# Three k pairs of each feed-forward down projection as seven block products

## What is computed

```python
def swiglu_ffn(h, w_in, w_out):
    g, u = jnp.split(h @ w_in, 2, axis=-1)
    return (jax.nn.silu(g) * u) @ w_out
...
    for l in range(DEPTH):
        x = x + 0.5 * swiglu_ffn(rmsnorm(x, norm_ffn1[l]), ffn1_w_in[l], ffn1_w_out[l])
        ...
        x = x + 0.5 * swiglu_ffn(rmsnorm(x, norm_ffn2[l]), ffn2_w_in[l], ffn2_w_out[l])
    return rmsnorm(x, norm_final)
```

## Time and profile before

| | us |
|---|---|
| median of three executions | 1100.32 (1100.07 to 1101.42) |
| the profiled execution, its own time | 1101.42 |
| its span, first to last instruction | 1099.6 |
| TensorE busy in the span | 1088.3 |
| VectorE busy | 727.4 |
| ScalarE busy | 547.6 |

### The profile page before, as it was taken

How to read it: one execution, slowest core, us unless ns; L and a number is a source line. 1 busy time by engine, 2 the same in 40 slices (tenths; PEclk the granted TensorE clock), 3 DMA queues, 4 the chain that set the end, 5 groups by cost and what they waited for, 6 DMA issues and landing times.

```text
span 1099.6 us, 14179 instructions
## 1 busy us (share of the span) xinstructions
PE 1088.3 (99%) x5350; PEld 919.9 (84%) x5350; DVE 727.4 (66%) x863; ACT 547.6 (50%) x616; POOL 394.8 (36%) x774
## 2 busy tenths in 40 slices
PE   8999999999999999999999999999999999999997
PEld 7878888889898888888888888888988988888886
DVE  6666556799776755655665665558997766666553
ACT  6453444854556545443454544357455645454432
POOL 0687632000000057673226858210000003686700
PEclk9999999999999999999999999999999999999999
DMA  8977566643553476765667776655455536766651
GB/s 277 290 226 230 181 205 210 213 170 134 210 192 114 142 224 216 219 213 204 210 205 218 217 222 201 203 198 196 149 178 184 175 121 193 216 216 221 204 192 66
DMA packets 183792, 215.92 MB, mean 196 GB/s; under 512 B 19088, under 2 KB 138540, under 8 KB 183724
## 3 DMA queue, kind: packets, MB, share of 16 engines
q1 hardware_dynamic: 158396, 200.55, 55.4%
q0 software_dynamic: 24064, 13.16, 4.4%
q10 hardware_dynamic: 1264, 1.32, 0.4%
HBM read 200.79 MB, written 1.05 MB: 184 GB/s over the span
## 4 chain that ended last, share of the span: by engine, by line
PE 93%; DMA 2%; DVE 2%; POOL 1%; ACT 1%; issue 1%; SPq 0%; ACTq 0%; DVEq 0%
PE acc L1497 26%; PE acc L1499 26%; PE acc L1498 26%; PE acc L1513 3%; PE acc L1514 3%; PE acc L1515 3%; PE turn L1374 2%; POOL kT L431 1%; DMA w_raw<-in_ffn_w_in 1%; DMA kT<-kT 1%; DVE w_lo L836 1%; ACT w_hi L470 1%; PE acc L1724 0%; PE acc L1723 0%; PE acc L1700 0%
## 5 line engine op out<-in xcount | busy, mean ns | idle before, releaser
L836 DVE TENSOR_TENSOR w_lo<-w_raw,w_hi 128x2048 fp32r<-128x2048 f32 (+1 forms) x190 | 426.0, 2246 | 194.9 <-ACT w_hi L470 194.8
L470 ACT CAST w_hi<-w_raw 128x2048 fp32r<-128x2048 f32 (+1 forms) x190 | 355.2, 1871 | 140.8 <-PE acc L1499 126.6
L431 POOL DMA_DIRECT2D kT<-kT x704 | 345.4, 499 | 161.6 <-DVE kT L968 120.8
L1497 PE MATMUL acc<-w_hi,xT 128*128 128x512 f32 x808 | 317.0, 392 | 0.7 <-DVE w_lo L836 0.6
L1499 PE MATMUL acc<-w_hi,xT 128*128 128x512 f32 x808 | 314.7, 390 | 0.0
L1498 PE MATMUL acc<-w_lo,xT 128*128 128x512 f32 x808 | 314.4, 389 | 0.0
L1497 PE MATMUL acc<-w_hi,hT 128*128 128x512 f32 x532 | 208.5, 392 | 0.0
L1499 PE MATMUL acc<-w_hi,hT 128*128 128x512 f32 x532 | 207.2, 390 | 0.0
L1498 PE MATMUL acc<-w_lo,hT 128*128 128x512 f32 x532 | 207.1, 389 | 0.0
L1497 PEld LDWEIGHTS acc<-w_hi,xT 128*128 128x128 f32 x808 | 151.7, 188 | 32.6 <-DVE w_lo L836 1.8
L1499 PEld LDWEIGHTS acc<-w_hi,xT 128*128 128x128 f32 x808 | 151.7, 188 | 31.8
(11 more groups left out here) (170 smaller groups left out, 951.9 us busy)
## 6 DMA issues: line engine op xcount, KB each, us to landing
w_raw<-in_ffn_w_in SPq DMA_DIRECT2D x172, 512.0 KB, 4.8
w_raw<-in_ffn_w_out SPq DMA_DIRECT2D x80, 512.0 KB, 4.4
w_raw<-in_mix_w_in SPq DMA_DIRECT2D x32, 512.0 KB, 4.5
w_raw<-in_xattn_wkv SPq DMA_DIRECT2D x32, 512.0 KB, 4.3
kT<-kT POOLq DMA_DIRECT2D x704, 16.0 KB, 3.3
w_raw<-in_mix_w_out SPq DMA_DIRECT2D x16, 512.0 KB, 4.4
w_raw<-in_xattn_wq SPq DMA_DIRECT2D x16, 512.0 KB, 4.6
w_raw<-in_xattn_wo SPq DMA_DIRECT2D x16, 512.0 KB, 4.5
```

Source lines behind the costliest of these rows:

```text
L431: pool.dma_start(hfeat[B * q:B * q + B, g % 2, a * RUN:(a + 1) * RUN], hblk[B * a:B * a + B, g % 2, q * RUN:(q + 1) * RUN]).then_inc(hfeat ...
L470: act.copy(w_hi[:, u % SLOTS, 0:n], w_raw[:, u % SLOTS, 0:n]).then_inc(w_split_hi, 1)
L836: dve.tensor_tensor(w_lo[:, u % SLOTS, 0:n], w_raw[:, u % SLOTS, 0:n], w_hi[:, u % SLOTS, 0:n].bitcast(F32), ALU.subtract).then_inc(w_spli ...
L1497: pe.matmul(o, hi, wh, start=(first and i == 0), stop=False)
```

## The change

For three pairs of k tiles (k 0 to 5) the two token tiles, the two k tiles and the two column halves make a 2 by 2 by 2 block product. Instead of eight block products (each three matmuls) seven are made, by Strassen's scheme in the form that shares sums. The list `DOWN` gives the new order of 15 units, here called D0 to D14 after their place in it: "singles" units hold two full weight rows of a pair (the four weight blocks, of which three are used directly, 9 matmuls), "sums" units hold four sums of blocks that VectorE makes out of the singles unit before (12 matmuls, no transfer), "rows" units are as before, with 4 or 2 k tiles. D1, D4 and D7 are singles, D2, D5 and D8 sums. All of n=0 ends with D9; n=1 is D10 to D14, with the two units of 2 k tiles as D11 and D12 and a unit of 4 k tiles last.

Sums over the tokens are made by VectorE in the first chunks (`token_sums`) and split by `sum_hi` and `sum_lo` into space of `xT` that is free after the in projection. The products that belong to several outputs are gathered by `shared_half`, `shares` and `last_shares`. The weight sums of the first pair stand in chunk 9, ahead of `hidden_lo`; in chunk 10 the block transpose now stands ahead of `split_lo` and `extra`.

```diff
+    SEVEN = 3
+    DOWN = [("rows", 0, 6, 4), ("singles", 0), ("sums", 0), ("rows", 0, 10, 4), ("singles", 1), ("sums", 1), ("rows", 0, 14, 4),
+            ("singles", 2), ("sums", 2), ("rows", 0, 18, 4), ("rows", 1, 6, 4), ("rows", 1, 18, 2), ("rows", 1, 20, 2),
+            ("rows", 1, 10, 4), ("rows", 1, 14, 4)]
+    U_MI = U_F1O + len(DOWN)
...
+            def square_parts(u, src, l, a):
+
+                return [(w_raw[:, u % SLOTS, i * 2 * GN:(i + 1) * 2 * GN], src[l, :, a + i, :]) for i in range(2)]
...
-                for n in range(2):
-                    for j in range(NGO):
-                        u = base + 2 * FC + n * NGO + j
-                        unit(u, at, wide_parts(u, src_out, l, GK * j, unit_kt(u), n * GN))
+                for i, e in enumerate(DOWN):
+                    u = base + 2 * FC + i
+                    if e[0] == "rows":
+                        unit(u, at, wide_parts(u, src_out, l, e[2], e[3], e[1] * GN))
+                    elif e[0] == "singles":
+                        unit(u, at, square_parts(u, src_out, l, 2 * e[1]))
+                    else:
+                        sp.wait_ge(w_split, at.at(UNITS, u + 1))
+                        sp.sem_inc(w_landed[u % SLOTS], 32)
...
+                f, e = down(u)
+                if e and e[0] == "sums":
+                    act.wait_ge(t_ready, at.at(2 * SEVEN, SEVEN * f + e[1] + 1))
+                else:
+                    act.wait_ge(w_landed[u % SLOTS], at.at(32 * (UNITS // SLOTS), 32 * (u // SLOTS + 1)))
                 act.wait_ge(unit_done, at.at(2 * UNITS, 2 * u + 2))
-                act.copy(w_hi[:, u % SLOTS, 0:n], w_raw[:, u % SLOTS, 0:n]).then_inc(w_split_hi, 1)
+                if e and e[0] == "singles":
+                    act.copy(w_hi[:, u % SLOTS, 0:GN], w_raw[:, u % SLOTS, 0:GN])
+                    act.copy(w_hi[:, u % SLOTS, 2 * GN:n], w_raw[:, u % SLOTS, 2 * GN:n]).then_inc(w_split_hi, 1)
+                else:
+                    act.copy(w_hi[:, u % SLOTS, 0:n], w_raw[:, u % SLOTS, 0:n]).then_inc(w_split_hi, 1)
...
+                    if c == FC - 1:
+                        sum_hi(0)
...
+                def sum_hi(p):
+                    at = Layer(l)
+                    act.wait_ge(s_sum_ready, at.at(2 * SEVEN, SEVEN * f + p + 1))
+                    act.wait_ge(unit_done, at.at(2 * UNITS, 2 * SLOTS + 2 * (base + 2 * FC - 1) + 2))
+                    act.copy(s_parts[p][:, :, 0, :], s_sum[p].rearrange("p (a s) -> p a s", a=2)).then_inc(s_hi_ready, 1)
+
                 for c in range(FC):
                     chunk(c, Layer(l))
-                split_hi(base + 2 * FC + 4, Layer(l))
+                state["next"] = base + 2 * FC + 4
+                for p in range(1, SEVEN):
+                    weights_to(base + 2 * FC + D_SUMS[p] - 1, Layer(l))
+                    sum_hi(p)
+                weights_to(base + 2 * FC + D_SUMS[-1], Layer(l))
...
+            def shared_half(f, at):
+
+                u = (U_F1O, U_F2O)[f] + D_SUMS[-1]
+                act.wait_ge(unit_done, at.at(2 * UNITS, 2 * SLOTS + 2 * u + 2))
+                act.wait_ge(s_ready, at.at(2 * SEVEN, SEVEN * f + SEVEN))
+                act.activation(shared, product_banks(f)[1][:, :], ACT.Copy, scale=0.5).then_inc(shared_ready, 1)
...
+                if e and e[0] == "singles" and e[1]:
+                    weight_sums(u, at)
...
+            def weight_sums(u, at):
+
+                w = w_raw[:, u % SLOTS, :].rearrange("p (i j n) -> p i j n", i=2, j=2)
+                s = w_raw[:, (u + 1) % SLOTS, :].rearrange("p (c n) -> p c n", c=4)
+                dve.wait_ge(w_landed[u % SLOTS], at.at(32 * (UNITS // SLOTS), 32 * (u // SLOTS + 1)))
+                dve.wait_ge(w_split, at.at(UNITS, SLOTS + u - 1))
+                steps.link(dve.tensor_tensor(s[:, 0:2, :], w[:, :, 1, :], w[:, 0, :, :], ALU.subtract))
+                steps.link(dve.tensor_tensor(s[:, 2, :], w[:, 1, 1, :], s[:, 0, :], ALU.subtract))
+                dve.tensor_tensor(s[:, 3, :], w[:, 1, 0, :], s[:, 2, :], ALU.subtract).then_inc(t_ready, 1)
...
-                    split_lo(base + 2 * c + 4, at)
-                    if (l, f) == (0, 0) and c in EXTRA:
-                        extra(EXTRA[c])
+                    def first_split():
+                        split_lo(base + 2 * c + 4, at)
+                        if (l, f) == (0, 0) and c in EXTRA:
+                            extra(EXTRA[c])
+
+                    if c < FC - 1:
+                        first_split()
...
+                    if c == FC - 2:
+                        weight_sums(base + 2 * FC + D_SUMS[0] - 1, at)
+                    if c == FC - 1:
+                        first_split()
+                        sum_lo(0)
...
+                    if c < SEVEN:
+                        token_sums(c, hfeat[:, g % 2, :].rearrange("p (a k t s) -> p k t a s", a=NBLK, k=2, t=T))
...
+                def token_sums(p, h):
+                    s = s_sum[p].rearrange("p (i a s) -> p i a s", i=4, a=NBLK)
+                    n = steps.mark(dve.tensor_tensor(s[:, 0, :, :], h[:, 0, 1, :, :], h[:, 1, 1, :, :], ALU.add))
+                    dve.tensor_tensor(s[:, 2, :, :], h[:, 0, 0, :, :], h[:, 0, 1, :, :], ALU.subtract)
+                    steps.wait(n)
+                    steps.link(dve.tensor_tensor(s[:, 1, :, :], s[:, 0, :, :], h[:, 0, 0, :, :], ALU.subtract))
+                    dve.tensor_tensor(s[:, 3, :, :], h[:, 1, 0, :, :], s[:, 1, :, :], ALU.subtract).then_inc(s_sum_ready, 1)
+
+                def sum_lo(p):
+                    dve.wait_ge(s_hi_ready, Layer(l).at(2 * SEVEN, SEVEN * f + p + 1))
+                    dve.tensor_tensor(s_parts[p][:, :, 1, :], s_sum[p].rearrange("p (a s) -> p a s", a=2),
+                                      s_parts[p][:, :, 0, :].bitcast(F32), ALU.subtract).then_inc(s_ready, 1)
+
                 for c in range(FC):
                     chunk(c, Layer(l))
-                split_lo(base + 2 * FC + 4, Layer(l))
+                state["next"] = base + 2 * FC + 4
+                for p in range(1, SEVEN):
+                    weights_to(base + 2 * FC + D_SUMS[p] - 1, Layer(l))
+                    sum_lo(p)
+                weights_to(base + 2 * FC + D_SUMS[-1], Layer(l))
                 hidden_lo(FC - 1)
-                state["next"] = base + 2 * FC + 5
...
+            def into_x(n, t, src, scalar):
+
+                o = xs[:, t, n * GN:(n + 1) * GN]
+                if scalar is None:
+                    return steps.mark(dve.tensor_tensor(o, src, o, ALU.add))
+                return steps.mark(dve.scalar_tensor_tensor(out=o, in0=src, scalar=scalar, in1=o, op0=ALU.mult, op1=ALU.add))
...
+            def shares(f, at):
+
+                u = (U_F1O, U_F2O)[f] + D_SUMS[-1]
+                m = product_banks(f)
+                dve.wait_ge(unit_done, at.at(2 * UNITS, 2 * SLOTS + 2 * u + 2))
+                dve.wait_ge(shared_ready, at.at(2, f + 1))
+                into_x(0, 0, shared, None)
+                steps.link(dve.scalar_tensor_tensor(out=shared_6, in0=m[6][:, :], scalar=0.5, in1=shared, op0=ALU.mult, op1=ALU.add))
+                steps.link(dve.scalar_tensor_tensor(out=shared, in0=m[7][:, :], scalar=0.5, in1=shared_6, op0=ALU.mult, op1=ALU.add))
+                steps.wait(into_x(0, 1, shared, None))
+
+            def last_shares(f):
+
+                m5 = product_banks(f)[5]
+                n = [into_x(1, 0, shared_6, None), into_x(1, 1, shared, None)]
+                for t in range(T):
+                    steps.wait(n[t])
+                    n[t] = into_x(1, t, m5[:, :], 0.5)
+                steps.wait(n[T - 1])
 
...
-                weights_to(U_F1O + 7, at)
-                update(0, 0, 0, U_F1O + 5, F1O_PAIR[0], 0.5, at)
-                update(0, 0, 1, U_F1O + 5, F1O_PAIR[0], 0.5, at)
+                weights_to(U_F1O + D_LAST[0] + 1, at)
+                shares(0, at)
+                weights_to(U_F1O + D_LAST[0] + 2, at)
+                update(0, 0, 0, U_F1O + D_LAST[0], F1O_PAIR[0], 0.5, at)
+                update(0, 0, 1, U_F1O + D_LAST[0], F1O_PAIR[0], 0.5, at)
                 for t in range(T):
                     x_blocks(2 * l, t)
-                weights_to(U_F1O + 11, at)
+                last_shares(0)
+                weights_to(U_MI, at)
                 gained_blocks(2 * l, G_MIX)
                 xT_lo_part(1, 0, 0, at)
                 xT_lo_part(1, 0, 1, at)
-                weights_to(U_MI, at)
-                update(0, 1, 0, U_F1O + 11, F1O_PAIR[1], 0.5, at)
+                update(0, 1, 0, U_F1O + D_LAST[1], F1O_PAIR[1], 0.5, at)
...
-                        ins = triple(acc[pair][t][:, :], u, j, t, 0, GN, False, t == 1 and j == GK - 1)
-                    ins.then_inc(unit_done, 1)
+                        ins = triple(acc[pair][t][:, :], u, j, t, 0, GN, False, False)
+                    if t == 0:
+                        ins.then_inc(unit_done, 1)
```

(67 more changed lines are left out.)

71 lines of the change are left out of this document (44 added, 27 removed).

## The result

The changed kernel takes 1103.6 us (median of 8, 1102.7 to 1105.7); the kernel before took 1100.9 us beside it on the same chip (8 runs, 1100.1 to 1101.4). The ratio is 1.0029, 95% interval 1.0020 to 1.0038. The forecast was 1095.9 us, with 1092.5 to 1099.8 as its range. The profiled execution took 1105.7 us, with a span of 1103.8 us against 1099.6. By the prediction's own sum the span should have shrunk by 4.4 us; it grew by 4.2, so 8.6 us have to be found.

A forecast was written before the change was run, and what follows sets the result against it. The prediction took TensorE's list of matmuls, busy 99% of the span, as the bound. Its terms, -8.2 + 2.6 + 1.8 + 0.1 - 0.7 = -4.4 us, gave 1095.9 us against the median of 1100.3, range 1092.5 to 1099.8.

The forecast's parts named there:

- No stall, but none to spare: At D3, D6 and D9, weight splits were to be ready in time, with margins of about 0.25 us.
- The landing that the prediction varied: Weight transfers' landing time, taken as 4.9 us for the later of two, with 4.4 and 5.3 as variations.
- The removed matmuls: In four down projections, 36 matmuls of 0.2267 us fall away on TensorE: 8.16 us saved.
- The `memT` wait: First feed-forward, chunk 10: `singles` waits for the fourth copy into `memT`, a stall of 2.6 us, once.
- D12: VectorE's dense list makes D12's split late: a 0.6 us stall in three feed-forwards, 1.8 us in all.
- Token sums: VectorE's four ops of 128 elements in each of chunks 0 to 2, 0.29 us each; about 0.1 us shows.
- The tail: Program's end: 18 matmuls, not 12, between the last two tiles' ends shorten the tail by 0.7 us.
- Rival 2: Late weight landings bring waits on TensorE: 1101.9 us at landings of 5.7 us, 1113.5 at 6.7; chance 0.16.
- Rival 3: VectorE's strided weight sums cost more than contiguous rows: 1099.1 us at 1.2 times, 1111 at twice; chance 0.14.
- landings of 5.3 us: Weight transfers landing in 5.3 us in place of 4.9 were said to move the sum to -2.6 us.
- Rival 1: All is hidden: the stalls at D12 and in chunk 10 vanish, giving 1091.4 us; chance 0.12.

The follow-up runs named there:

- e5: The kernel of e2, with SyncE issuing D4's weight transfer only when D2's split is done; 1099.3 us in one execution.
- e1: The changed kernel with 13 matmuls, whose result nobody reads, ahead of TensorE's wait for `memT`; 1102.5 us, ratio 1.0015.
- e3: The changed kernel with `hidden_hi(9)` and `hidden_lo(9)` in chunk 10 moved behind D3's rounding and remainder; 1099.0 us, ratio 0.9979.
- e11: The changed kernel with one edit, GpSimd's select (mask of the gate matrices) one shuffle earlier; 1102.5 us, ratio 1.0017.
- e10: The kernel of e9, with GpSimd's select (mask of the gate matrices) one shuffle earlier; 1094.1 us, ratio 0.9938, the fastest of all.
- e7: The kernel before, with only the change's order of the second column half (two-tile unit second, not last) and its split of the last four tiles; 1100.3 us, ratio 0.9990.
- e12: The kernel of e10, with the next stage's first-half blocks ahead of its first weight split at each feed-forward end; 1103.5 us, ratio 1.0026.
- e9: The changed kernel with e2's and e3's moves, e3's order in chunk 9 too, and the first token sums split before D2's weights; 1096.5 us, ratio 0.9966.
- e2: The changed kernel with chunk 10's copy into `memT` ahead of the transpose and D2's split; 1102.7 us, ratio 1.0012.
- e6: The changed kernel with chunk 10's block transpose back behind D2's split and the `memT` copy; 1103.7 us in one execution.

## Why the prediction was wrong

The step that failed is the one at D3: "No stall, but none to spare". Its arithmetic of the weight chain stood, but it left out what stands ahead of D3's rounding on ScalarE, `hidden_hi(9)`, and with it a landing that the change itself moves. No stop was predicted there; it measured 5.1 us. The landing that the prediction varied was that of the weights; the one that decided was that of the small pieces behind them (e5). Term by term, in the two profiled spans:

- **The removed matmuls**: 36 x 0.2267 = 8.2 us. Right.
- **The `memT` wait**: 2.6 predicted, 3.1 beyond the pace measured. The mechanism and nearly the size were right. What it set off was not in the sum: 2.9 us at half clock, a term that the prediction put at nothing and gave no reason for. e1 shows the cause. In the executions of e3 and e11 the same fall was shorter and cost 1.6 us, so the profiled execution, 2 us above the median, may owe over 1 us of that to it.
- **D3**: 0 predicted, 5.1 measured in this execution, shown by e3 (the order) and e5 (the transfer).
- **D12**: 1.8 predicted, nothing measured in the changed kernel. Here the list was too dear: VectorE began D12's split at 542.59 and ended it 1.22 us later, 44.15 us behind D0's start if the stop at D3 is taken off (543.81 - 497.90 - 1.76), and not 44.8, against the 44.2 at which TensorE wants it.
- **Token sums**: 0.29 us each, as predicted. Their place, beside GpSimd's select, was the cost. D0 of the first feed-forward begins 0.6 us later than before (135.39 against 134.82), where 0.1 was expected. e10 and e11 show it.
- **The tail**: -0.7 predicted, -1.1 measured, all of it from the order (e7).
- The rest, some 1.8 us, is what is left over: 1.4 us in the four down stages, 0.4 between them. Stops of 0.1 to 0.3 us at D6, D9 and the `x_turn` transposes are among it. It was not taken apart.

Together 0.5 + 2.9 + 5.1 - 1.8 + 0.5 - 0.4 + 1.8 = 8.6, the 8.6 us missing; it closes because the last term is a remainder. Rival 2 (late landings) had the kind of wait and the sign, but with another transfer. Rival 3 fell: the sums cost what contiguous rows do. (Its price at twice was also mis-added: 5 us in each of four feed-forwards are 20 us, not 15; and landings of 5.3 us give -2.9, not -2.6. Nothing hung on either.) Rival 1's time, 1091.4 us, is what is left to reach: e10 comes to 1094.1 with the same matmuls, and its largest waits after the start are 1.6 us at one `x_turn` and 0.4 at two splits. Not all of e10's 6.6 us is the block products': the tail's order gains in the kernel before too (e7), and what the earlier select would give there was not run. Their own worth shows in the stages: from D0's first matmul to the next stage's first, the first feed-forward of each layer takes 58.5 and 58.4 us in e10 (134.36 to 192.82, 672.49 to 730.92) where it took 60.3 and 60.2 (134.82 to 195.13, 673.66 to 733.86), 1.8 us of the 2.04 that 9 matmuls cost. So the block products were worth nearly what they seemed; the order of the helper queues around them was what failed.

## What to carry to other kernels

When a change makes one step of a fixed queue shorter, list every transfer that this frees earlier, and ask which small transfers are being issued at that moment on another queue: they may land behind it. Work whose input comes by such a transfer should stand behind the splits that TensorE wants next, unless something needs it sooner (e3: 4.7 us for a change of order; e12: 9 us lost by the opposite order, falls of the clock included). And the price of a new wait on TensorE is the wait plus what the clock may do behind it, so a new wait of about 3 us is to be priced at up to twice its length until a trace says otherwise: the clock's part here was 2.9 us once and 1.6 us twice.

## What was unexpected of the hardware

- **The clock behind a wait.** After 2.92 us idle the granted clock was 0.50 until 150.2. After 1.78 us idle in e9 it was 0.50 too (73.5 to 76.8); after 1.84 us in e11 and 1.71 us in the changed kernel it stayed at 1.00, and so it did after 2.40 us behind 735.91 in e12. The length of the stop alone does not tell it in these runs. In the tail of the kernel before, with no matmul after 1091.71, it was still 1.00 over 1093 to 1097 and 0.52 over 1097 to 1099.
- **Small pieces behind a big transfer.** 16 pieces of 16 KB, the last taken up 1.1 to 1.2 us behind its issue when the 512 KB transfer is issued after them (the kernel before, e5) and 3.0 to 4.7 us when it is issued before the last of them (the changed kernel, e1, e2, e6, e11; three later feed-forwards each).
- **VectorE beside GpSimd.** A select of 128x1024 on GpSimd lengthened two VectorE operations by 0.9 us each, one of them of 0.29 us. The Trainium skill (SBUF — State Buffer, on who interferes with whom) says that a VectorE instruction with two SBUF inputs contends with a GpSimd instruction that reads SBUF; e10 agrees, with 0.29 and 2.29 us once they are apart.
